# Attention steps of a two-block transformer kernel: six or eight probability slots instead of four, another order on VectorE and ScalarE, and a tile's normalisation one step later

## What is computed

```
logits = einsum('bnqgrd,bnkgd->bngrqk', qb, kb) * (HEAD_DIM ** -0.5)
logits = where(mask, logits, -inf)
p = softmax(concatenate([logits, sink], axis=-1), axis=-1)[..., :-1]
o = einsum('bngrqk,bnkgd->bnqgrd', p, vb)
...
y_a = o_a @ w_branch_a;  y_b = o_b @ w_branch_b
mix = sigmoid(g_a) * y_a + sigmoid(g_b) * y_b
```

## Time and profile before

| what | value |
|---|---|
| median of 3 runs | 1589.59 us (1589.38 to 1591.28) |
| the profiled execution's own time | 1589.65 us |
| its span in the profile | 1587.9 us |
| attention stage in the trace | about 1062.3 to 1162.9 us |
| TensorE busy over the span | 1569.8 us (99%) |
| VectorE, ScalarE, GpSimd busy | 772.8, 505.3 and 709.4 us |

### The profile page before, as it was taken

One profiled execution on the slowest core, in us unless ns is written; L12 is line 12 of the kernel. 1 busy time (PEld: TensorE's weight loads), 2 busy tenths in 40 slices (PEclk: granted clock), 3 DMA queues, 4 the chain that ended last, 5 costly groups with the idle time before them and its releaser, 6 DMA issues.

```text
span 1587.9 us, 19582 instructions
## 1 busy us (share of the span) xinstructions
PE 1569.8 (99%) x7591; PEld 1295.6 (82%) x7591; DVE 772.8 (49%) x1111; ACT 505.3 (32%) x750; POOL 709.4 (45%) x273
## 2 busy tenths in 40 slices
PE   9999999999999999999999999998999999999998
PEld 6887788888888988888888887876678988888886
DVE  5901588910166566666104389987573431023203
ACT  3012211210125444344224344237543432124312
POOL 5875189677771344544442002421143244344451
PEclk9999999999999999999999999999999999999999
DMA  6232032232333233233233222231133122223221
GB/s 226 82 131 80 1 113 80 81 128 83 106 106 106 82 105 105 80 106 106 82 105 114 72 90 79 81 80 28 28 107 133 54 85 101 106 81 105 106 89 71
DMA packets 123286, 147.00 MB, mean 93 GB/s; under 512 B 5144, under 2 KB 98376, under 8 KB 123209
## 3 DMA queue, kind: packets, MB, share of 16 engines
q1 hardware_dynamic: 121334, 141.05, 27.9%
q10 hardware_dynamic: 1874, 4.85, 1.0%
HBM read 143.79 MB, written 2.10 MB: 92 GB/s over the span
## 4 chain that ended last, share of the span: by engine, by line
PE 94%; POOL 2%; DVE 1%; issue 1%; DMA 1%; ACT 1%; SPq 0%; DVEq 0%; POOLq 0%; ACTq 0%
PE ps L655 29%; PE ps L657 28%; PE ps L656 28%; PE ps L810 3%; PE ps L885 2%; PE ps L1052 1%; POOL w_lo L608 1%; PE ps L873 1%; PE ps L1069 1%; POOL w_hi L603 1%; PE ps L944 1%; PE ps L906 0%; DMA raw<-in_w_in 0%; DMA raw<-in_w_up 0%; DVE probs L1939 0%
## 5 line engine op out<-in xcount | busy, mean ns | idle before, releaser
L608 POOL TENSOR_TENSOR w_lo<-raw,w_hi 128x1024 fp32r<-128x1024 f32 x224 | 558.3, 2513 | 711.9 <-ACT w_hi L1117 709.1
L655 PE MATMUL ps<-hT_hi,w_hi 128*128 128x512 f32 (+1 forms) x928 | 355.7, 383 | 0.8 <-POOL w_lo L608 0.5
L656 PE MATMUL ps<-hT_lo,w_hi 128*128 128x512 f32 (+1 forms) x928 | 354.4, 382 | 0.0
L657 PE MATMUL ps<-hT_hi,w_lo 128*128 128x512 f32 (+1 forms) x928 | 354.3, 382 | 0.0
L1117 ACT ACTIVATE w_hi<-raw 128x2048 fp32r<-128x2048 f32 (+1 forms) x87 | 165.0, 1896 | 241.8 <-PE ps L655 211.1
L655 PEld LDWEIGHTS ps<-hT_hi,w_hi 128*128 128x128 f32 x928 | 174.4, 188 | 36.8 <-issue 2.3
L657 PEld LDWEIGHTS ps<-hT_hi,w_lo 128*128 128x128 f32 x928 | 174.4, 188 | 34.0
L656 PEld LDWEIGHTS ps<-hT_lo,w_hi 128*128 128x128 f32 x928 | 174.5, 188 | 33.4
L603 POOL TENSOR_TENSOR w_hi<-raw,cells 128x2048 fp32r<-128x2048 f32 x35 | 129.5, 3701 | 126.5 <-PE ps L655 125.1
L657 PE MATMUL ps<-w_hi,f_lo 128*128 128x512 f32 x400 | 155.6, 389 | 0.0
L655 PE MATMUL ps<-w_hi,f_hi 128*128 128x512 f32 x400 | 155.6, 389 | 0.0
(11 more groups left out here) (312 smaller groups left out, 2184.5 us busy)
## 6 DMA issues: line engine op xcount, KB each, us to landing
raw<-in_w_in SPq DMA_DIRECT2D x86, 512.0 KB, 4.6
raw<-in_w_up SPq DMA_DIRECT2D x76, 512.0 KB, 4.6
raw<-in_w_down SPq DMA_DIRECT2D x54, 512.0 KB, 4.1
raw<-in_w_out SPq DMA_DIRECT2D x16, 512.0 KB, 4.1
raw<-in_w_ret_o SPq DMA_DIRECT2D x8, 512.0 KB, 4.0
raw<-in_w_sgu_o SPq DMA_DIRECT2D x8, 512.0 KB, 4.0
x<-in_x SPq DMA_DIRECT2D x4, 512.0 KB, 6.2
raw<-in_w_branch_b SPq DMA_DIRECT2D x4, 512.0 KB, 6.3
```

What stands on the lines that cost most here:

```text
L608: nc.gpsimd.tensor_tensor(lo[:, c], raw[:, s, c], hi[:, c].bitcast(f32), ALU.subtract).then_inc(unit_split, 1)
L655: first = nc.tensor.matmul(dst, a_hi, b_hi, start=start, stop=False)
L656: nc.tensor.matmul(dst, a_hi, b_lo, start=False, stop=False)
L657: return first, nc.tensor.matmul(dst, a_lo, b_hi, start=False, stop=stop)
```

## The change

The slots of the window branch hold 256 columns and there are eight; those of the second branch hold 512 and there are six, at an address that reaches into the 4 KB of `qT_b` and `kT_b`, which are no longer read by then. Logits s wait for the transpose of head s-6 instead of s-4. On VectorE, even steps now start with the logits, then the copy of the transpose, then the rest; `later` moves each `out_T` into the following step, behind the logits and ahead of `o_split`. On ScalarE `o_split` goes to the end of its step. The split of `oTb` starts two heads later. TensorE's order stays.

```
--- before.py
+++ after.py
@@ -88,6 +88,16 @@
     return [e for step in ATTENTION for e in sorted(step, key=rank)]
 
 
+def later(kind, ranks):
+
+    steps = [[] for _ in range(len(ATTENTION) + 1)]
+    for p, step in enumerate(ATTENTION):
+        for e in sorted(step, key=lambda e: ranks[p % 2].get(e[0], 4)):
+            steps[p + (e[0] == kind)].append(e)
+    return [e for p, step in enumerate(steps)
+            for e in sorted(step, key=lambda e: 3 if e[0] == kind else ranks[p % 2].get(e[0], 4))]
+
+
 def has_ticket(kind, n):
     if kind == "part":
         return part_of(n)[2] == part_of(n)[3] - 1
@@ -96,8 +106,8 @@
 
 ATTENTION = attention_steps()
 EVENTS = [e for step in ATTENTION for e in step]
-ACT_EVENTS = in_order(lambda e: 0 if e[0] in ("probs_T", "out_T", "o_split") else 1)
-DVE_EVENTS = in_order(lambda e: {"probs_T": 0, "sums": 1, "logits": 2}.get(e[0], 3))
+ACT_EVENTS = in_order(lambda e: {"probs_T": 0, "out_T": 1, "o_split": 3}.get(e[0], 2))
+DVE_EVENTS = later("out_T", {0: {"logits": 0, "probs_T": 1, "sums": 2}, 1: {"probs_T": 0, "sums": 1, "logits": 2}})
 TICKETED = [e for e in EVENTS if has_ticket(*e)]
 RETENTION = [("scores", 0), ("scores", 1), ("values", 0), ("scores", 2), ("values", 1),
              ("scores", 3), ("values", 2), ("values", 3)]
@@ -128,6 +138,7 @@
 
 T0, N_TICKETS = starts(TICKETS)
 ROTATING, COLUMN_BANK, VALUES_BANK = 5, 5, 6
+PROBS_B, PROBS_A = 8, 6
 LATE_COLUMNS = ((1, KT - 2), (1, KT - 1))
 
 
@@ -195,7 +206,7 @@
 G_B = [T0["g_b_0"], T0["g_b_1"], T0["g_b_2"]] + [T0["g_b_3"] + n for n in range(5)]
 G_A = [T0["g_a"] + c for c in range(GA_IN)] + [column_ticket(0, c) for c in range(GA_IN, KT)]
 Y_B = [column_ticket(1, c) for c in range(KT)]
-OTB_AT = 38
+OTB_AT = 40
 HI_AT = {1: U0["y_b"], GA_PARTS + 1: U0["y_b"] + 1, GA_PARTS + 9: U0["y_a"]}
 
 
@@ -338,7 +349,8 @@
         kT_a = at("kT_a", [P, S], B2 + 20 * KB)
         qT_b = at("qT_b", [P, NT, S], B2 + 22 * KB)
         kT_b = at("kT_b", [P, S], B2 + 30 * KB)
-        probs = at("probs", [P, 4, S], B2 + 32 * KB)
+        probs_b = at("probs_b", [P, 8, 2 * P], B2 + 32 * KB)
+        probs_a = at("probs_a", [P, PROBS_A, S], B2 + 28 * KB)
         score3 = at("score3", [P, S], B2 + 32 * KB)
         work = at("work", [P, S], B2 + 34 * KB)
         score2 = at("score2", [P, 3 * P], B2 + 36 * KB)
@@ -374,6 +386,10 @@
         spare = {(phase, n): [at(f"{part}_{phase}_{n}", [P, UNIT], A + k * KB, f32r)
                               for part, k in zip(("spare_hi", "spare_lo"), pair)]
                  for phase, pairs in spare_at.items() for n, pair in enumerate(pairs)}
+
+        def probs_of(s):
+
+            return probs_b[:, s % PROBS_B, :] if s < NT * HEADS else probs_a[:, s % PROBS_A, :]
 
         def slot_of(u):
 
@@ -1053,7 +1069,7 @@
                                      k[r, k0 * P:(tt + 1) * P], start=True, stop=True).then_inc(psum_ready, 1)
                 elif kind == "probs_T":
                     pe.wait_ge(probs_made, s + 1)
-                    transposes(event("probs_T", s), [probs[:, s % 4, n * P:(n + 1) * P] for n in range(nk)])
+                    transposes(event("probs_T", s), [probs_of(s)[:, n * P:(n + 1) * P] for n in range(nk)])
                 elif s % 2 == 0:
                     value = dsa_value if branch else swa_value
                     b = VALUES_BANK + turn % 2
@@ -1403,7 +1419,7 @@
                     if s % HEADS == 0 and turn >= 2:
                         act.wait_ge(ri_made, turn - 1)
                     await_evacuated(act, event("logits", s))
-                    nc.scalar.activation(probs[:, s % 4, 0:nk * P], probs[:, s % 4, 0:nk * P], ACT.Exp,
+                    nc.scalar.activation(probs_of(s)[:, 0:nk * P], probs_of(s)[:, 0:nk * P], ACT.Exp,
                                          bias=nm[:, turn % 2, h:h + 1], scale=-1.0,
                                          accum_out=rs[:, turn % 2, h:h + 1]).then_inc(probs_made, 1)
                     if s % HEADS == HEADS - 1 and turn < NT:
@@ -1933,10 +1949,10 @@
                         added, least = mask[:, tt, 0:nk * P], -LOWEST
                     else:
                         added, least = band[:, (2 - nk) * P:2 * P], nsink[:, h:h + 1]
-                    if s >= 4:
-                        await_psum(dve, event("probs_T", s - 4))
+                    if s >= 6:
+                        await_psum(dve, event("probs_T", s - 6))
                     await_psum(dve, t)
-                    V.tensor_tensor_reduce(out=probs[:, s % 4, 0:nk * P], in0=ps[:, BANK[t], 0:nk * P], in1=added,
+                    V.tensor_tensor_reduce(out=probs_of(s)[:, 0:nk * P], in0=ps[:, BANK[t], 0:nk * P], in1=added,
                                            scale=-(HD ** -0.5), scalar=least, op0=ALU.add, op1=ALU.min,
                                            accum_out=nm[:, turn % 2, h:h + 1]).then_inc(evacuated[BANK[t]], 1)
                     if s % HEADS == HEADS - 1 and not branch:
```

## The result

The changed kernel took 1595.0 us (median of 7 executions, 1594.67 to 1597.31), the kernel before 1589.59 us (7 executions beside it, 1589.3 to 1591.28). The ratio is 1.0037, 95% interval 1.0026 to 1.0047: slower by more than the 0.2% that count as no change. The forecast was 1592.7 with a range up to 1594.9, so the loss was forecast, and the time lies 0.1 us above the range. So what went wrong is better read from the terms of the sum than from the total.

A forecast was written before the change was run, and what follows sets the result against it. TensorE, 99% of the span, was taken to bound the kernel, so reordering gains only in its idle time: 2.8 us gained early, 1.9, 1.5, 2.4 and 0.1 lost late, +3.1 us, 1592.7 us, range 1588.2 to 1594.9.

The forecast's parts named there:

- up to step 11: Early attention steps: some 0.8 us gained by step 6, only 0.3 kept because GpSimd's weight split sets the end.
- steps 12, 13: Attention stage, before T23: the bank of L24 is freed earlier, removing TensorE's 0.60 us wait; gain 0.5 us.
- steps 14 to 17: Attention stage: the 0.85 us wait before T31 goes and L34's slow start shrinks by an estimated 0.1; gain 1.0 us.
- steps 20 to 22: Split of oTb: VectorE waits for ScalarE, TensorE some 2.3 us for L43 and 0.7 for T43, equal to old losses: 0.
- step 23, column 1: Normalisation moved behind the reductions: out_T, oTa_hi, oTa_lo, gate in one chain, oTa_lo held by GpSimd; loss 1.9 us.
- step 27, column 3: Same chain of out_T, oTa_hi, oTa_lo and gate after the reductions delays column 3 to 1142.9; loss 1.5 us.
- step 31, column 6: oTa_lo asked for half a microsecond too late, held by GpSimd, with T60's copy and column 6 behind; loss 2.4 us.
- The lock at step 9: VectorE's second small add ends only with GpSimd's second weight-split instruction, so GpSimd's old clock sets this stretch's end.
- The late chains: Steps 23, 27, 31 and 35: out_T, oTa_hi, oTa_lo and gate in one step; losses 1.9, 1.5, 2.4, 0.1 us.
- Rival (3): GpSimd's lock is missed in step 31 or step 23: 1590.4 to 1591.4 us, both 1589.1; chance 0.22.
- Rival (2): Steps 20 to 22: each later oTb_lo also waits for its oTb_hi, total +4.7 us, 1594.3 us; chance 0.18.
- theory A: From the experiments: chains cost about +3.1 us; each wait of about 2 us before a column can lower the clock, 1.5 us.

The follow-up runs named there:

- the slots alone: Changed kernel with out_T and o_split back in their old places and oTb split from head 38, keeping slots and early logits reductions: 1587.22 us, ratio 0.9985.
- the kernel of the parts that pay: Slots and early logits without the normalisation move, oTb_lo subtractions spread out, two later weight units started clear of VectorE's subtractions: 1583.64 us, ratio 0.9962 to the kernel before.
- the gates first: Changed kernel with the gates of steps 23 and 27 directly behind the logits reductions, ahead of out_T and oTa_lo: 1590.84 us, ratio 1.0007.
- the fills: Changed kernel with useless matmuls in TensorE's waits: long ones before columns 1 and 3, 1599.05 us; shorter ones before columns 1, 3 and 6, 1594.49 us.

## Why the prediction missed

**The step that failed** is the sum itself: "-2.8 + 1.9 + 1.5 + 2.4 + 0.1 = +3.1". It takes the granted clock of 1.00 as given while it makes three new waits of 2 us, and has no term for what a wait does to the matmuls behind it: +1.6 us in this profile. The terms, measured between the same TensorE starts in the two profiled executions (the stage starts 0.15 us later in the changed kernel, which is taken off):

| term | forecast | measured |
|---|---|---|
| up to step 11 | -0.3 | -0.85 |
| steps 12, 13 | -0.5 | -0.2 |
| steps 14 to 17 | -1.0 | -0.55 |
| steps 18, 19 | -1.0 | -1.05 |
| steps 20 to 22 | 0 | 0 |
| step 23, column 1 | +1.9 | +2.1 |
| step 27, column 3 | +1.5 | +1.6 |
| low clock behind column 3 | none | +1.6 |
| step 31, column 6 | +2.4 | +2.3 |
| step 35 | +0.1 | +0.1 |
| sum | +3.1 | +5.0 |

Without the low clock the forecast's own terms measure +3.4 us. Of the 2.3 us between 1592.7 and 1595.0, 1.6 are the low clock, 0.3 the terms, and the rest, some 0.35 us, lies ahead of and behind the stage.

**The front of the stage.** Its sum was right (2.65 for 2.8), but partly by luck: 0.55 us more than forecast up to step 11 and 0.75 less in steps 12 to 17 nearly cancel. The bank waits went as said: none before T31 and T34, 0.16 us before T23. I had too little for the first steps and too much for 12 to 17, where the logits groups at 1090.48 and 1096.27 now take 1.44 and 1.38 us for 1.13 and 1.02. The lock at step 9 held VectorE through a copy (wide_ri, 2.30 us at 1081.36) rather than through the second add; the copy ended with GpSimd's second instruction:

```profile
1078.67 4.71 POOL L624 TENSOR_TENSOR w_lo<-raw,w_hi 128x1024 fp32r<-128x1024 f32 x2 [25.10 <-ACT w_hi L1133]
...
1081.36 2.30 DVE L1984 COPY wide_ri<-cells 128x512 f32<-128x512 f32 x1
```

In steps 20 to 22 the mechanism was as told, an idle VectorE of 2.40 us before the first oTb_lo, with 1.47 us of TensorE's wait for the 2.3 forecast and 0.37 for 0.7; the zero stands. But the prediction put the wait down to `OTB_AT`, and the slots alone, with the old `OTB_AT`, show the same 1.47 us.

**The late chains** were right in place, in order and within 0.2 us in size, and both bets on GpSimd held: 1.93 us in step 23, 2.38 in step 31. From the first y_b part to y_a the stage grew by 7.6 us for the 5.9 forecast; 1.6 of the 1.7 more are the low clock. The Trainium skill, SBUF — State Buffer, section "Who interferes with whom", calls the shared port pair an exclusive lock that goes by issue order; the traces agree, and moving GpSimd alone brought oTa_lo from 2.38 back to 0.69 us. Rival (3) is out by this. Rival (2) is out too: the later oTb_lo came at 1114.64, 1116.02 and 1117.14, the one wait among them for ScalarE 0.22 us. Its time, 1594.3, was close for another reason.

**The clock.** Four kinds of evidence stand for theory A. First, in the profiles every stretch in the attention stage but the fall inside the 11.28 and 8.10 us of idle time begins within 1.5 us behind a wait: eleven behind waits of 1.89 to 3.40 us, four behind the early wait of 0.86 us. Second, the times stand in groups about 1.5 us apart, with the mean granted clock falling by about 0.001 a group. Third, the same fall came in the old order when VectorE was made late, in all five executions by their times. Fourth, none came behind the columns in the profile where they were filled. Read as numbers of stretches, the groups give 0.3 an execution for the kernel before, 0.4 for the slots alone and 0.2 for the kernel of the parts that pay, none of which has a wait over 1.5 us, and 1.4 for the changed kernel.

Against a simple rule stand three things. Nine other waits of 1.93 to 3.02 us were passed at 1.00, so of twenty long waits barely more than half brought a stretch; the early wait of 0.86 us was followed by one in four profiles of thirteen. With the gates first, one long wait of three is left, and still there are 1.3 stretches an execution. And the fills, meant to settle it, did not move the median (0.8 stretches an execution by the groups). What decides whether a given wait brings the clock down stays open: its length, the idle time around it or the moment at which it falls were not told apart, and it is not shown that idle time alone is the cause. With no stretch the changed kernel would take about 1593.0 to 1593.4 us (1594.52 or 1595.0 less 1.6, an estimate), 0.3 to 0.7 above the forecast and inside its range.

One sign lay open beforehand: three executions of the kernel before spread over 1.9 us, 1589.38 to 1591.28, far more than a kernel bound by its instruction order has reason to. I read that as noise. Those three have no profile, but in the later sets the upper group at about 1591 has a mean clock of mostly 0.998, and the lower one 0.999 or 1.0, so it was most likely one stretch more.

## What to carry to other kernels

A wait on the engine that bounds the kernel costs its length and can cost more behind it: here eleven of twenty waits of 1.9 to 3.4 us brought some 1.6 us of slower matmuls. The three kernels whose waits all stayed under 1.5 us ran without a stretch in most executions, the changed kernel in none. Where times of one kernel come in groups, price the step between groups before pricing the change. Freeing a buffer earlier and moving work later are two edits: here one was worth -2.4 us and the other +9.7 alone (with two stretches in its profile; together they came to +5, so the two do not add up), and only running them apart showed that the first was worth keeping.
